# A hybrid encoder layer on one core: the first stage reordered by token tile and weight quarter, three latent units in full float32

## The chip, the core and the metric

The kernel runs on one core of one Trainium2 chip. The metric is the device time of one execution in microseconds (us), as the median of several runs; smaller is better. TensorE (PE in the profile, with its weight loads as PEld) multiplies, VectorE is DVE, ScalarE is ACT, GpSimd is POOL, and SyncE (SP) issues most of the loads. Each engine works through its own instructions in the order in which they are written, and waits at semaphores for the others.

## The reference, cut to what matters

One layer of a streaming encoder for 512 prompt tokens and 32 sample tokens, width 1024:

```python
xn = rms_norm(x, g_mix_norm)
z = xn @ w_in
c_q, c_kv, k_r, u, gate_a, gate_b = jnp.split(z, IN_SPLITS, axis=-1)   # 256, 128, 32, 1024, 1024, 1024
...
attn = chunk_causal_mla(q_nope, q_rope, k_nope, kr_all, v, q_pos, ...)
rec, h_last = rg_lru(u_c, h0, w_rg, b_rg, w_ig, b_ig, lru_lambda)
mixed = jax.nn.sigmoid(gate_a) * attn + jax.nn.sigmoid(gate_b) * rec
x = x + mixed @ w_out
up = rms_norm(x, g_ffn_norm) @ w_up
up_c, ffn_buf_new = causal_dwconv(up, ffn_buf, ffn_conv_w, ffn_conv_b)
gate, val = jnp.split(up_c, 2, axis=-1)
x = x + (jax.nn.silu(gate) * val) @ w_down
```

The first 416 columns of `w_in` give the latents (`c_q`, `c_kv`, `k_r`); only their product is touched here. `rg_lru` needs softplus(-lru_lambda), one small vector.

## The kernel before

Most products are made with three float32r matmuls in place of one float32 matmul: each operand is split into a high part (rounded to float32r) and a low part (the rest), and high x high, low x high and high x low are added up in PSUM. ACT makes the high parts and DVE the low ones by subtraction.

The first stage computes the latents of five token tiles: four of 128 prompt tokens and one that holds the 32 sample tokens. The product over the 1024 inputs runs in eight steps k of 128, and two steps share one load of weights, a weight quarter (128 x 832). A token tile times a weight quarter is called a unit here: twenty units, of 2 x 3 matmuls with 416 columns each. In `before.py` the stage goes so:

- SP (lines 386 to 412) issues the identity and the norm's gain, the five loads of `x` (512 KB for a prompt tile), weight quarters 0 and 1, thirteen loads of small vectors, and quarters 2 and 3, into `raw`. The weights of later items (512 KB) follow in `w_in_item`, each waiting for an earlier low split.
- PE transposes all of x tile by tile (`x_transpose`, line 1637), ACT and DVE each copy half of every tile to `xT` (`xT_left`, line 1142), and PE fills its wait with `keep_clock(7, 11)`, matmuls without use.
- ACT and DVE then split x times the gain, k by k over all tokens (`x_hi`, `x_lo`), and the weight quarters (`split_hi`, `split_lo`).
- PE multiplies quarter by quarter (line 1678), over all five tiles in each. After quarter 0 it transposes the small vectors (`vectors_transpose`), and after quarter 2 it spreads the inverse root mean squares over the partitions (line 1690).
- ACT's sums of squares of x (line 722) go to DVE, which makes the inverse roots (lines 1156 to 1157) and the diagonal tiles `dgx` (line 1159). The spread of them goes from PSUM to `rsT` (lines 1163 and 1164), and then `s_rs` is raised. After that comes the split of the first later item, and then the chain of 27 small instructions for softplus (lines 1171 to 1184).

The next stage on PE begins with

```python
pe.wait_ge(s_rs, 1)
pe.wait_ge(s_vec, 2)
for g, (kind, n) in enumerate(FIRST):
    ...
    product(xnh, xnl, g % 2, [(I_IN + g, I_IN + g, 0, KD)], None, early_keys(g), 5)
```

and `product` waits for the item's low split (`s_lo`). Everything later is released in turn from these products.

Of the kernel before, what the change touches and what calls it, by code (L numbers as in the profile page):

```python
# [15 lines left out]
F32 = mybir.dt.float32  # L16
# [4 lines left out]
P = 128  # L21

D = 1024
# [113 lines left out]
def layer(nc, i, c, o):  # L137
# [3 lines left out]
    with ctx:  # L141
# [33 lines left out]
        U = fixed("U", [P, KD, LEAD + TU])  # L175
        gates = fixed("gates", [P, 3, 2, T])
# [55 lines left out]
        lsq = at("lsq", [P, NTT, KVL + ROPE], zone + NTT * QL * 4)  # L232
        mxh = at("mxh", [P, KD, T], xs, F32R)
# [70 lines left out]

        def sem(name):
            return ctx.enter_context(nc.semaphore(name))
# [3 lines left out]
        s_xt = [sem(f"x{t}_in") for t in range(NTT)]  # L310
# [14 lines left out]
        s_xTd, s_xTa, s_xTv = sem("x_transposed"), sem("xT_left_half"), sem("xT_right_half")  # L325
# [59 lines left out]
        def _(sp):  # L385
            sp.dma_start(ident[:, :], c["ident"]).then_inc(s_ident, 16)
            sp.dma_start(vrows[V_GMIX:V_GMIX + 8, 0, :], i["g_mix_norm"].rearrange("a (m p) -> (a m) p", p=P)).then_inc(s_gain, 16)
            for t, (c0, p0, n) in enumerate(TOK):
                src = i["x_prompt"][0, c0:c0 + n, :] if t < NT else i["x_sample"][0]
                sp.dma_start(xnat[p0:, t, :], src).then_inc(s_xt[t], 16)  # L390
# [19 lines left out]

            latent_weights(2)
            latent_weights(3)
# [30 lines left out]

            for t in range(I_IN, I_IN + 11):
                w_in_item(t)
# [65 lines left out]
        def _(pool):  # L511
            step = Count(s_pool)

            pool.wait_ge(s_xt[NT], 16)
# [156 lines left out]
        def _(act):  # L671
# [5 lines left out]
            def split_hi(t, slot, loaded, n=KD * P):  # L677

                act.wait_ge(s_w[slot % 4], loaded)
                if not isinstance(t, int) or t >= 2:  # L680
                    act.wait_ge(s_used, t - 1)
                nc.scalar.activation(hi[:, slot % 2, 0:n], raw[:, slot % 4, 0:n], ACT.Copy).then_inc(s_hi, 1)  # L682
# [13 lines left out]
            def xT_left(t):  # L696
                c0, _, n = TOK[t]
                act.wait_ge(s_xTd, t + 1)
                nc.scalar.activation(xT[:, 0:4, c0:c0 + n], PS[:, 2 * (t % 2), :].rearrange("p (k n) -> p k n", k=4)[:, :, 0:n],
                                     ACT.Copy).then_inc(s_xTa, 1)  # L700

            def x_hi(dst, k, g0):

                nc.scalar.activation(dst[:, k, :], xT[:, k, :], ACT.Copy, scale=vec[:, g0 + k:g0 + k + 1]).then_inc(s_xh, 1)

            act.wait_ge(s_vecT, 1)
            nc.scalar.activation(vec[:, 0:8], PS[:, 6, 0:8], ACT.Copy).then_inc(s_vec, 1)
            for t in range(NTT):
                xT_left(t)
            act.wait_ge(s_vec, 1)  # L710
            act.wait_ge(s_xTa, NTT)
            act.wait_ge(s_xTv, NTT)
            for k in range(KD):
                x_hi(xnh, k, V_GMIX)
                if k in (0, 2):
                    split_hi(k // 2, k // 2, 16, 2 * LAT)

            act.wait_ge(s_cpre, 1)
            for t, (c0, p0, n) in enumerate(TOK):
# [3 lines left out]
                if t == 1:  # L723
                    split_hi(2, 2, 16, 2 * LAT)
# [4 lines left out]
            split_hi(3, 3, 16, 2 * LAT)  # L729
            split_hi(I_IN, I_IN, 32)  # L730
# [9 lines left out]
            split_hi(I_IN + 1, I_IN + 1, 32)  # L740
# [364 lines left out]
        def _(dve):  # L1105
# [34 lines left out]
            for t, (c0, _, n) in enumerate(TOK):  # L1140
                dve.wait_ge(s_xTd, t + 1)
                nc.vector.tensor_copy(xT[:, 4:8, c0:c0 + n], PS[:, 2 * (t % 2) + 1, :].rearrange("p (k n) -> p k n", k=4)[:, :, 0:n]).then_inc(s_xTv, 1)

            def x_lo(high, low, k, g0, count):

                dve.wait_ge(s_xh, count + k + 1)
                stt(low[:, k, :], xT[:, k, :], vec[:, g0 + k:g0 + k + 1], high[:, k, :].bitcast(F32), ALU.mult, ALU.subtract).then_inc(s_xl, 1)

            for k in range(KD):
                x_lo(xnh, xnl, k, V_GMIX, 0)  # L1150
                if k in (0, 2):
                    split_lo(k // 2, k // 2, 2 * LAT)
            split_lo(2, 2, 2 * LAT)
# [31 lines left out]


# [272 lines left out]
            split_item(I_IN + 1)  # L1459
# [81 lines left out]
            for m in range(KD):  # L1541
                x_m = xT[:, m, :]
                dve.wait_ge(s_used, I_OUT + m + 1)
                tt(halves(x_m), up_pair(m % 4), halves(x_m), ALU.add).then_inc(s_free, 1)
                dve.wait_ge(s_xh, KD + m + 1)
# [68 lines left out]
        def _(pe):  # L1614
# [22 lines left out]
            def x_transpose(t):  # L1637
                _, p0, n = TOK[t]
                pe.wait_ge(s_xt[t], 16)
                if t >= 2:  # L1640
                    pe.wait_ge(s_xTa, t - 1)
                    pe.wait_ge(s_xTv, t - 1)
                for k in range(KD):
                    last = nc.tensor.transpose(PS[:, 2 * (t % 2) + k // 4, (k % 4) * P:(k % 4) * P + n],  # L1644
                                               xnat[p0:, t, k * P:(k + 1) * P], ident[p0:, p0:])
                last.then_inc(s_xTd, 1)

            def vectors_transpose():

                pe.wait_ge(s_rows, 16 * 13)  # L1650
                pe.wait_ge(s_xTa, NT)
                pe.wait_ge(s_xTv, NT)
                for a, (c0, n) in enumerate(((0, V_N), (V_N, 2 * NU), (V_N + 2 * NU, 2 * NU), (V_N + 4 * NU, 2 * NU))):
                    last = nc.tensor.transpose(PS[:, 2, c0:c0 + n], vrows[0:n, a, :], ident[0:n, 0:n])
                last.then_inc(s_vecT, 1)

            pe.wait_ge(s_ident, 16)
            pe.wait_ge(s_gain, 16)
            nc.tensor.transpose(PS[:, 6, 0:8], vrows[0:8, 0, :], ident[0:8, 0:8]).then_inc(s_vecT, 1)
            for t in range(NTT):  # L1660
                x_transpose(t)
# [6 lines left out]
            keep_clock(7, 11)  # L1668

            for t4 in range(4):  # L1670
                pe.wait_ge(s_lo, t4 + 1)
                for kk, t in [(kk, t) for kk in range(2) for t in range(NTT)] if t4 < 3 else [(kk, t) for t in range(NTT) for kk in range(2)]:
                    k = 2 * t4 + kk
                    pe.wait_ge(s_xl, k + 1)
                    w0 = TOK[t][0] - TOK[t][1]
                    cols = slice(kk * LAT, (kk + 1) * LAT)
                    for w, x in ((hi, xnh), (hi, xnl), (lo, xnh)):
                        last = mm(PS[:, 3 + t, 0:LAT], x[:, k, w0:w0 + P], w[:, t4 % 2, cols],  # L1678
                                  start=(k == 0 and w is hi and x is xnh), stop=(k == KD - 1 and w is lo))
                    if t4 == 3 and t < NT and kk:  # L1680
                        last.then_inc(s_latp, 1)
                last.then_inc(s_used, 1)
                if t4 == 0:
                    vectors_transpose()
                if t4 == 2:

                    pe.wait_ge(s_rsn, 1)
                    for t, (c0, p0, n) in enumerate(TOK):
                        dst = PS[:, 0, c0:c0 + n] if t < NT else PS[:, 1, 0:n]
                        last = mm(dst, ones[:, :], dgx[:, t, p0:p0 + n], start=True, stop=True)  # L1690
                    last.then_inc(s_rsb, 1)
# [348 lines left out]
            for r in range(4):  # L2040
# [5 lines left out]
                product(x2h, x2l, r, [(I_UP + r, r, 0, KD)], (s_xl, KD) if r == 0 else None, x2_sums if r == 0 else None)  # L2046
# [109 lines left out]
```

## Time and profile before

| what | value |
|---|---|
| median of 3 runs | 859.44 us (859.42 to 859.92) |
| the profiled execution | 859.77 us |
| its span, first to last instruction | 857.5 us |
| PE busy | 841.3 us, 98% |
| DVE, ACT, POOL busy | 572.4, 365.2, 199.1 us |
| mean granted TensorE clock | 0.999 |

All times of rows are microseconds from the start of the span. The span leaves 2.3 us of the execution outside. A row of a group of instructions gives their busy time and the mean duration of one; a busy engine can start its next instruction before the record of the last has ended.

### The profile page before, as it was taken

How to read it: one execution, taken by the hardware profiler on the slowest of the kernel's cores; microseconds unless marked ns; L12 is line 12 of the kernel's file. 1: busy time of each engine (PE TensorE's matmuls, PEld its weight loads, DVE VectorE, ACT ScalarE, POOL GpSimd, SP SyncE). 2: the span in 40 equal slices, each digit the busy share in tenths (PEclk: the TensorE clock that was granted, in tenths of full speed). 3: DMA queues.
4: the chain of work that ended last, by engine and by line, in shares of the span. 5: the costliest groups of instructions: out<-in, count | busy, mean ns of one | idle time of the engine just before them, and what ended most of it. 6: DMA issues, size and time to landing. Idle time of an engine off the chain costs nothing.

```text
span 857.5 us, 16853 instructions
## 1 busy us (share of the span) xinstructions
PE 841.3 (98%) x6564; PEld 806.9 (94%) x6564; DVE 572.4 (67%) x1056; ACT 365.2 (43%) x608; POOL 199.1 (23%) x228
## 2 busy tenths in 40 slices
PE   7999999899999999999999999999999999999998
PEld 7999899789999899877999999999999999999998
DVE  5686678877676676887655888878888886222121
ACT  6635959755645556557245222222222221222121
POOL 4021123202111121121140444333442344010000
PEclk9999999999999999999999999999999999999999
DMA  8434211131120200100223233232323223233321
GB/s 256 112 91 109 78 51 39 40 81 38 33 58 18 53 26 28 50 2 26 75 75 99 74 99 92 79 98 73 98 79 92 86 79 93 83 106 103 105 57 40
DMA packets 114466, 63.73 MB, mean 74 GB/s; under 512 B 7660, under 2 KB 112878, under 8 KB 114412
## 3 DMA queue, kind: packets, MB, share of 16 engines
q1 hardware_dynamic: 112428, 59.25, 24.2%
q0 software_dynamic: 1936, 3.70, 1.7%
q8 instruction: 38, 0.62, 0.3%
q14 instruction: 16, 0.13, 0.0%
q10 hardware_dynamic: 48, 0.02, 0.0%
HBM read 59.85 MB, written 2.70 MB: 73 GB/s over the span
## 4 chain that ended last, share of the span: by engine, by line
PE 88%; ACT 6%; DVE 3%; issue 2%; DMA 0%; SPq 0%; ACTq 0%; DVEq 0%
PE PS L1632 49%; PE PS L1785 9%; PE PS L1868 6%; PE PS L1840 4%; PE PS L1802 4%; PE PS L1678 3%; PE PS L1744 2%; PE PS L1822 2%; PE PS L2075 2%; PE PS L1776 2%; PE PS L1740 1%; PE PS L1766 1%; PE PS L1707 1%; PE PS L1644 1%; PE PS L1847 1%
## 5 line engine op out<-in xcount | busy, mean ns | idle before, releaser
L682 ACT ACTIVATE w_hi<-w_raw 128x1024 fp32r<-128x1024 f32 (+2 forms) x102 | 105.4, 1034 | 301.4 <-PE PS L1632 288.8
L1115 DVE TENSOR_TENSOR w_lo<-w_raw,w_hi 128x1024 fp32r<-128x1024 f32 (+2 forms) x102 | 127.2, 1247 | 103.6 <-ACT w_hi L682 103.5
L1632 PE MATMUL PS<-x2h,w_hi 128*128 128x272 f32 x704 | 145.7, 288 | 0.0
L1632 PE MATMUL PS<-x2h,w_lo 128*128 128x272 f32 x704 | 145.7, 288 | 0.0
L1632 PE MATMUL PS<-x2l,w_hi 128*128 128x272 f32 x704 | 145.1, 288 | 0.0
L1632 PEld LDWEIGHTS PS<-x2h,w_hi 128*128 128x128 f32 x704 | 110.8, 188 | 0.1
L1632 PEld LDWEIGHTS PS<-x2l,w_hi 128*128 128x128 f32 x704 | 110.6, 189 | 0.0
L1632 PEld LDWEIGHTS PS<-x2h,w_lo 128*128 128x128 f32 x704 | 109.9, 189 | 0.0
L643 POOL TENSOR_TENSOR uct<-uct 128x512 f32<-128x512 f32 x22 | 28.4, 1292 | 165.0 <-DVE uct L1585 165.0
L1632 PE MATMUL PS<-hh,w_hi 128*128 128x272 f32 x308 | 64.2, 289 | 0.0
L1632 PE MATMUL PS<-hh,w_lo 128*128 128x272 f32 x308 | 63.8, 288 | 0.0
L1632 PE MATMUL PS<-hl,w_hi 128*128 128x272 f32 x308 | 63.5, 288 | 0.0
L1785 PE MATMUL PS<-xnh,w_hi 128*128 128x272 f32 x192 | 57.2, 298 | 0.2 <-DVE KT L1294 0.2
L1785 PE MATMUL PS<-xnh,w_lo 128*128 128x272 f32 x192 | 55.6, 290 | 0.0
L1785 PE MATMUL PS<-xnl,w_hi 128*128 128x272 f32 x192 | 55.2, 287 | 0.0
L901 ACT ACTIVATE PT<-PS 128x128 f32<-128x128 f32 (+4 forms) x72 | 31.3, 435 | 51.9 <-PE PS L1822 48.4
L574 POOL TENSOR_TENSOR rot<-Qn,rope 128x320 f32<-128x320 f32 x16 | 14.9, 949 | 160.5 <-DVE Qn L1284 160.5
L1802 PE MATMUL PS<-KT,QT 100*128 100x128 f32 (+3 forms) x128 | 46.9, 448 | 3.5 <-ACT Pn L887 2.2
L1632 PEld LDWEIGHTS PS<-hl,w_hi 128*128 128x128 f32 x308 | 48.4, 189 | 0.0
L1632 PEld LDWEIGHTS PS<-hh,w_hi 128*128 128x128 f32 x308 | 48.3, 188 | 0.1
L1632 PEld LDWEIGHTS PS<-hh,w_lo 128*128 128x128 f32 x308 | 48.1, 189 | 0.0
L1840 PE MATMUL PS<-PT,V 128*128 128x128 f32 x320 | 47.0, 278 | 0.0
(295 smaller groups left out, 1865.1 us busy)
## 6 DMA issues: line engine op xcount, KB each, us to landing
w_raw<-in_w_up_dram SPq DMA_DIRECT2D x44, 512.0 KB, 3.8
w_raw<-in_w_in_dram SPq DMA_DIRECT2D x24, 512.0 KB, 3.8
w_raw<-in_w_down_dram SPq DMA_DIRECT2D x16, 512.0 KB, 3.6
w_raw<-in_w_out_dram SPq DMA_DIRECT2D x8, 512.0 KB, 3.6
w_raw<-in_w_down_dram SPq DMA_DIRECT2D x8, 384.0 KB, 3.9
xnat<-in_x_prompt_dram SPq DMA_DIRECT2D x4, 512.0 KB, 5.0
w_raw<-in_w_in_dram SPq DMA_DIRECT2D x4, 416.0 KB, 6.5
wq<-in_w_q_b_dram SPq DMA_DIRECT2D x8, 192.0 KB, 2.5
```

Of the source, the lines that this page charges most:

```text
L643: nc.gpsimd.tensor_tensor(h_j[:, 0:SEQ], uct[:, j, 0:SEQ], h_j[:, 0:SEQ], ALU.mult)
L682: nc.scalar.activation(hi[:, slot % 2, 0:n], raw[:, slot % 4, 0:n], ACT.Copy).then_inc(s_hi, 1)
L901: nc.scalar.activation(PT[:, b, 0:w], PS[:, 6 + b, 0:w], ACT.Copy).then_inc(s_ptf, 1)
L1115: tt(lo[:, slot % 2, 0:n], raw[:, slot % 4, 0:n], hi[:, slot % 2, 0:n].bitcast(F32), ALU.subtract).then_inc(s_lo, 1)
L1632: last = mm(joined_half(2 * rank, j), w[:, slot % 2, cols], x[:, k0 + k, j * HT:(j + 1) * HT], start=(k0 + k == 0 and first), stop=(k0 + k ...
L1678: last = mm(PS[:, 3 + t, 0:LAT], x[:, k, w0:w0 + P], w[:, t4 % 2, cols], start=(k == 0 and w is hi and x is xnh), stop=(k == KD - 1 and w ...
L1744: last = mm(bank[:, a * 2 * QK:(a + 1) * 2 * QK], cqT[:, k, c0 - p0:c0 - p0 + P], wq[:, q % 2, k, :], start=(k == 0), stop=(k == NQ - 1))
L1776: last = mm(PS[:, bank, a * P:(a + 1) * P], latT[:, k0:k0 + P], wkv[:, q % 2, 1, :], start=True, stop=True)
L1785: last = mm(PS[:, j, 0:HT], w[:, item % 2, cols], x[:, k, j * HT:(j + 1) * HT], start=(k == 0 and first), stop=(k == KD - 1 and w is lo))
L1802: mm(bank[:, 0:w], QT[0:QK + NT, 2 * par + h, t * P:(t + 1) * P], KT[0:QK + NT, 2 * par + h, 0:w], start=True, stop=True).then_inc(s_s, 1)
L1840: last = mm(values_bank(h)[:, t * P:(t + 1) * P], V[:, par, a, h:h + 2, :].rearrange("p h n -> p (h n)"), PT[:, b, a * P:(a + 1) * P], sta ...
L1868: last = mm(PS[:, 2 * (r % 4) + j, 0:HT], w[:, cols], x[:, k, j * HT:(j + 1) * HT], start=(k == 0 and first), stop=(k == KD - 1 and w is w ...
```

## The change

The twenty units are ordered by tile and quarter, so that work starts on the first tile while the others load. x is first multiplied by the gain into `xg` (two tile slots) and split tile by tile, in seven parts: tiles 0 and 1 in halves, tiles 2, 3 and the sample tile whole. `xT` is filled by ACT alone (`x_kept`). The weight quarters have split tiles of their own (`lw_hi`, `lw_lo`). The three units (0,0), (1,0) and (0,1) (tile, quarter) multiply `xg` and `raw` in full float32, two matmuls each, and need no split. The two first later items are split ahead of the stage's end, and the copies to `rsT` come after softplus.

```diff
@@ SP
+            load_x(0, 0, D // 2)
             latent_weights(0)
+            load_x(0, D // 2, D)
+            load_x(1, 0, D // 2)
+            load_x(1, D // 2, D)
             latent_weights(1)
+            load_x(2)
+            latent_weights(2)
+            load_x(3)
+            load_x(4)
+            latent_weights(3)
...
+            sp.wait_ge(s_whole, 3)
             for t in range(I_IN, I_IN + 11):
                 w_in_item(t)
@@ ACT
+            def x_hi(part):
+                t, k0, k1 = XPARTS[part]
+                act.wait_ge(s_xg, part + 1)
+                nc.scalar.activation(x_tile(xnh, t, k0, k1), xg[:, t % 2, k0:k1, 0:TOK[t][2]], ACT.Copy).then_inc(s_xgh, 1)
+            def x_kept(t):
+                act.wait_ge(s_xTd, parts_of(t))
+                nc.scalar.activation(x_tile(xT, t, 0, KD), x_columns(t, 0, KD), ACT.Copy).then_inc(s_xTa, 1)
+            def latent_split_hi(q):
+                act.wait_ge(s_w[q], 16)
+                nc.scalar.activation(lw_hi[:, q, :], raw[:, q, 0:2 * LAT], ACT.Copy).then_inc(s_hi, 1)
...
+            x_hi(0)
+            latent_split_hi(0)
+            x_hi(1)
+            x_hi(2)
+            latent_split_hi(1)
+            x_hi(3)
+            x_kept(0)
+            x_kept(1)
+            x_hi(4)
+            latent_split_hi(2)
+            act.wait_ge(s_cpre, 1)
+            squares(0)
+            x_kept(2)
+            x_hi(5)
+            squares(1)
+            x_kept(3)
+            x_hi(6)
+            x_kept(4)
+            latent_split_hi(3)
+            for t in range(2, NTT):
+                squares(t)
+            split_hi(I_IN, I_IN, 32)
+            split_hi(I_IN + 1, I_IN + 1, 32)
@@ DVE
+            def x_scaled(part):
+                t, k0, k1 = XPARTS[part]
+                n = TOK[t][2]
+                dve.wait_ge(s_xTd, part + 1)
+                if t in (2, 3):
+                    dve.wait_ge(s_whole, 3)
+                gain = vec[:, V_GMIX + k0:V_GMIX + k1].unsqueeze(2).to_broadcast([P, k1 - k0, n])
+                tt(xg[:, t % 2, k0:k1, 0:n], x_columns(t, k0, k1), gain, ALU.mult).then_inc(s_xg, 1)
+            def x_lo(part):
+                t, k0, k1 = XPARTS[part]
+                dve.wait_ge(s_xgh, part + 1)
+                tt(x_tile(xnl, t, k0, k1), xg[:, t % 2, k0:k1, 0:TOK[t][2]], x_tile(xnh, t, k0, k1).bitcast(F32),
+                   ALU.subtract).then_inc(s_xgl, 1)
...
+            x_scaled(0)
+            x_lo(0)
+            x_scaled(1)
+            latent_split_lo(0)
+            x_scaled(2)
+            x_lo(2)
+            latent_split_lo(1)
+            x_scaled(3)
+            x_lo(1)
+            x_lo(3)
+            x_scaled(4)
+            x_lo(4)
+            latent_split_lo(2)
+            x_scaled(5)
+            x_lo(5)
+            x_scaled(6)
+            x_lo(6)
+            latent_split_lo(3)
...
-            split_lo(3, 3, 2 * LAT)
-            dve.wait_ge(s_rsb, 1)
-            nc.vector.tensor_copy(rsT[:, 0:SEQ], PS[:, 0, :])
-            nc.vector.tensor_copy(rsT[:, S0:], PS[:, 1, 0:DEC]).then_inc(s_rs, 1)
             split_lo(I_IN, I_IN)
+            split_lo(I_IN + 1, I_IN + 1)
 
             dve.wait_ge(s_spe, 1)
...
             ts(la_s[:, :], acc, -8.0, None, ALU.mult).then_inc(s_sp, 1)
 
+            dve.wait_ge(s_rsb, 1)
+            nc.vector.tensor_copy(rsT[:, 0:SEQ], PS[:, 0, :])
+            nc.vector.tensor_copy(rsT[:, S0:], PS[:, 1, 0:DEC]).then_inc(s_rs, 1)
@@ PE
+            def latent_product(t, q):
+                w0 = TOK[t][0] - TOK[t][1]
+                if t in (3, 4):
+                    pe.wait_ge(s_xg, parts_of(3))
+                    pe.wait_ge(s_xTa, 4)
+                for kk in range(2):
+                    k = 2 * q + kk
+                    pe.wait_ge(s_xgl, part_with(t, k) + 1)
+                    pe.wait_ge(s_hi, q + 1)
+                    cols = slice(kk * LAT, (kk + 1) * LAT)
+                    for w, x in ((lw_hi, xnh), (lw_hi, xnl), (lw_lo, xnh)):
+                        if w is lw_lo:
+                            pe.wait_ge(s_lo, q + 1)
+                        last = mm(PS[:, 3 + t, 0:LAT], x[:, k, w0:w0 + P], w[:, q, cols], ...)
...
+            def whole_latent_product(t, q):
+                pe.wait_ge(s_w[q], 16)
+                for kk in range(2):
+                    k = 2 * q + kk
+                    pe.wait_ge(s_xg, part_with(t, k) + 1)
+                    last = mm(PS[:, 3 + t, 0:LAT], xg[:, t, k, :], raw[:, q, kk * LAT:(kk + 1) * LAT], start=k == 0, stop=False)
+                last.then_inc(s_whole, 1)
...
+            keep_clock(5, 3)
+            x_transpose(0)
+            keep_clock(5, 2)
+            whole_latent_product(0, 0)
+            x_transpose(1)
+            keep_clock(5, 2)
+            x_transpose(2)
+            x_transpose(3)
+            whole_latent_product(1, 0)
+            whole_latent_product(0, 1)
+            latent_product(1, 1)
+            x_transpose(4)
+            latent_product(0, 2)
+            latent_product(1, 2)
+            for q in range(3):
+                latent_product(2, q)
+            x_transpose(5)
+            x_transpose(6)
+            for q in range(3):
+                latent_product(3, q)
+            vectors_transpose()
+            for t in range(4):
+                latent_product(t, 3)
+            latent_product(4, 0)
+            latent_product(4, 1)
+            x_rms_spread()
+            latent_product(4, 2)
+            latent_product(4, 3)
```

`x_transpose(part)` waits, from part 4 on, for the scaled parts and the kept copy (`s_xTa`) of the tile two before, because tiles 0, 2 and 4 share two PSUM banks and tiles 1 and 3 two others. Bank 6 of tile 3's columns is also the bank of its latents.

## Rows read from the trace of the kernel before

**Rows 1.** The page: busy time of the engines.
```profile
PE 841.3 (98%) x6564; PEld 806.9 (94%) x6564; DVE 572.4 (67%) x1056; ACT 365.2 (43%) x608; POOL 199.1 (23%) x228
```

**Rows 2.** The chain that ended last, 0 to 80 us: start, duration, what.
```profile
5.38 6.00 PE PS L1644 x32
...
15.12 5.91 PE PS L1678 x30
21.04 0.33 PE PS L1654 x4
21.37 11.33 PE PS L1678 x60
32.70 1.03 PE PS L1690 x10
...
39.49 6.01 PE PS L1632 x48
45.49 0.44 PE PS L1715 x4
...
74.56 1.85 PE PS L1707 x8
```

**Rows 3.** PE's timeline: start, duration, instructions.
```profile
2.90 0.24 PE L1659 MATMUL PS<-ident,vrows 8*128 8x8 f32 x1 [2.90 <-DMA vrows<-in_g_mix_norm_dram]
...
11.96 2.72 PE L1666 MATMUL PS<-ident 128*128 128x128 f32 x22
...
39.32 0.42 PE L1632 MATMUL PS<-xnh,w_hi 128*128 128x272 f32 x2
```

**Rows 4.** Stretches: length, busy (records) of PE, PEld, DVE, ACT, POOL, PEclk, DMA, GB/s.
```profile
5.00:10.00 5.00, 4.62 (x22) 4.62 (x23) 1.38 (x2) 1.19 (x2) 0.00 (x0) 1.00 1.04 361
...
10.00:11.00 1.00, 1.00 (x11) 1.00 (x10) 0.47 (x1) 0.47 (x1) 0.36 (x1) 1.00 1.02 379
```

**Rows 5.** Loads issued in two short stretches: KB, us from issue to landing.
```profile
xnat<-in_x_prompt_dram SPq DMA_DIRECT2D x1, 512.0 KB, 3.7
...
w_raw<-in_w_in_dram SPq DMA_DIRECT2D x1, 416.0 KB, 7.9
```

**Rows 6.** Groups by line and shape, 5 to 40 us: busy us, mean ns.
```profile
L1115 DVE TENSOR_TENSOR w_lo<-w_raw,w_hi 128x832 fp32r<-128x832 f32 x4 | 4.1, 1021 | 1.4 <-ACT w_hi L682 1.4
L682 ACT ACTIVATE w_hi<-w_raw 128x832 fp32r<-128x832 f32 x4 | 3.5, 887 | 0.7 <-PE PS L1678 0.7
...
L1142 DVE COPY xT<-PS 128x512 f32<-128x512 f32 x4 | 2.8, 692 | 8.3 <-PE PS L1644 8.3
...
L699 ACT ACTIVATE xT<-PS 128x512 f32<-128x512 f32 x4 | 2.4, 598 | 6.3 <-PE PS L1644 6.3
...
L1115 DVE TENSOR_TENSOR w_lo<-w_raw,w_hi 128x1024 fp32r<-128x1024 f32 x1 | 1.2, 1214 | 0.0
...
L682 ACT ACTIVATE w_hi<-w_raw 128x1024 fp32r<-128x1024 f32 x1 | 1.1, 1057 | 4.7 <-PE PS L1678 4.7
```

**Rows 7.** ACT's timeline, two sums of squares.
```profile
22.20 1.04 ACT L722 ACTIVATE junk<-xnat 128x1024 f32<-128x1024 f32 x1
...
23.36 1.06 ACT L722 ACTIVATE junk<-xnat 128x1024 f32<-128x1024 f32 x1
```

**Rows 8.** DVE's timeline from the squares to the first product's evacuation.
```profile
25.72 0.17 DVE L1156 TENSOR_SCALAR small<-small 128x5 f32<-128x5 f32 x1 [2.37 <-ACT junk L722]
...
27.93 1.07 DVE L1159 TENSOR_SCALAR dgx<-ident,small 128x128 f32<-128x128 f32 x5
...
35.61 0.19 DVE L1171 RECIPROCAL small<-la_s 128x8 f32<-128x8 f32 x1
...
40.94 0.17 DVE L1184 TENSOR_SCALAR la_s<-small 128x8 f32<-128x8 f32 x1
...
47.29 0.72 DVE L1453 TENSOR_TENSOR gates<-PS,rsT 128x544 f32<-128x544 f32 x1
```

**Rows 9.** PE's waits from 60 us on: us in total, times, longest.
```profile
PE PS L1802 <- ACT Pn L887: 2.2, 2, 1.2
```

More of the change, by code:

```diff
@@ L175, in layer @@
         U = fixed("U", [P, KD, LEAD + TU])
+        gates_at = place
         gates = fixed("gates", [P, 3, 2, T])
@@ L303, in score_bank, with parts_of, part_with, x_columns @@
             return PS[:, 2 + 2 * ((p + n) % 2), :]
+        XPARTS = [(0, 0, 4), (0, 4, 8), (1, 0, 4), (1, 4, 8)] + [(t, 0, 8) for t in range(2, NTT)]
+        def parts_of(t):
+            return sum(part[0] <= t for part in XPARTS)
+        def part_with(t, k):
+            return [k0 <= k < k1 and tile == t for tile, k0, k1 in XPARTS].index(True)
+        def x_columns(t, k0, k1):
+            bank = 6 if t in (1, 3) else 0
+            return PS[:, bank:bank + 2, :].rearrange("p a (k n) -> p (a k) n", k=4)[:, k0:k1, 0:TOK[t][2]]
+        def x_tile(x, t, k0, k1):
+            c0, _, n = TOK[t]
+            return x[:, k0:k1, c0:c0 + n]
         def sem(name):
@@ L309, in layer @@
         s_gain = sem("mix_gain_in")
-        s_xt = [sem(f"x{t}_in") for t in range(NTT)]
+        s_xt = [sem(f"x{t}_{k0}_in") for t, k0, _ in XPARTS]
         s_w = [sem(f"w{s}_in") for s in range(4)]
@@ L693, in rsqrt_guess, with squares @@
                 nc.scalar.activation(dst, dst, ACT.Exp, scale=-0.5).then_inc(sem_, 1)
[L696 to L719, printed above, removed]
+            def x_hi(part):
[8 more added lines that the diff above has]
+                nc.scalar.activation(lw_hi[:, q, :], raw[:, q, 0:2 * LAT], ACT.Copy).then_inc(s_hi, 1)
+            def squares(t):
+                _, p0, _ = TOK[t]
                 if t:
@@ L1138, in _, with latent_split_lo @@
             nc.vector.memset(small[0:LASTP, 2, NT:NTT], 1.0).then_inc(s_cpre, 1)
[L1140 to L1153, printed above, removed]
+            def x_scaled(part):
[11 more added lines that the diff above has]
+                   ALU.subtract).then_inc(s_xgl, 1)
+            def latent_split_lo(q):
+                dve.wait_ge(s_hi, q + 1)
+                tt(lw_lo[:, q, :], raw[:, q, 0:2 * LAT], lw_hi[:, q, :].bitcast(F32), ALU.subtract).then_inc(s_lo, 1)
+            dve.wait_ge(s_vec, 1)
+            x_scaled(0)
[16 more added lines that the diff above has]
+            latent_split_lo(3)
             dve.wait_ge(s_ss, NTT)
@@ L1458, in _ @@
             link(nc.vector.tensor_reduce(small[:, 0, 2 * NTT:3 * NTT], lsq[:, :, KVL:], X, ALU.add))
-            split_item(I_IN + 1)
             latent_norms()
@@ L1634, in product, with x_transpose, keep_clock @@
                     last.then_inc(s_used, 1)
-            def x_transpose(t):
+            def x_transpose(part):
+                t, k0, k1 = XPARTS[part]
                 _, p0, n = TOK[t]
-                pe.wait_ge(s_xt[t], 16)
+                pe.wait_ge(s_xt[part], 16)
                 if t >= 2:
+                    pe.wait_ge(s_xg, parts_of(t - 2))
                     pe.wait_ge(s_xTa, t - 1)
[L1642 to L1645, printed above, removed]
+                for k in range(k0, k1):
+                    last = nc.tensor.transpose(x_columns(t, k, k + 1)[:, 0], xnat[p0:, t, k * P:(k + 1) * P], ident[p0:, p0:])
                 last.then_inc(s_xTd, 1)
+            def keep_clock(bank, count):
+                for _ in range(count):
+                    mm(PS[:, bank, 0:P], ident[:, :], ident[:, :], start=True, stop=True)
             def vectors_transpose():
                 pe.wait_ge(s_rows, 16 * 13)
-                pe.wait_ge(s_xTa, NT)
-                pe.wait_ge(s_xTv, NT)
+                pe.wait_ge(s_vec, 1)
                 for a, (c0, n) in enumerate(((0, V_N), (V_N, 2 * NU), (V_N + 2 * NU, 2 * NU), (V_N + 4 * NU, 2 * NU))):
@@ new lines, in whole_latent_product, with x_rms_spread @@
+            def whole_latent_product(t, q):
[5 more added lines that the diff above has]
+                last.then_inc(s_whole, 1)
+            def x_rms_spread():
+                pe.wait_ge(s_rsn, 1)
+                for t, (c0, p0, n) in enumerate(TOK):
+                    dst = PS[:, 0, c0:c0 + n] if t < NT else PS[:, 1, 0:n]
+                    last = mm(dst, ones[:, :], dgx[:, t, p0:p0 + n], start=True, stop=True)
+                last.then_inc(s_rsb, 1)
@@ L1657, in _ @@
             pe.wait_ge(s_ident, 16)
             pe.wait_ge(s_gain, 16)
-            nc.tensor.transpose(PS[:, 6, 0:8], vrows[0:8, 0, :], ident[0:8, 0:8]).then_inc(s_vecT, 1)
-            for t in range(NTT):
-                x_transpose(t)
-            def keep_clock(bank, count):
-                for _ in range(count):
-                    mm(PS[:, bank, 0:P], ident[:, :], ident[:, :], start=True, stop=True)
[L1668 to L1691, printed above, removed]
```

40 lines of the change are left out of this document (25 added, 15 removed).

## The prediction

> **What bounds the kernel now.** First the page's busy times: PE is busy 98% of the span [rows 1], so a change of this stage is worth what it does to the moment at which PE starts the next one. Then the chain that ended last, over the first 80 us. The reader is to see that it hardly leaves PE: transposes of x from 5.38, the latent products from 15.12, the small vectors and the spread of the inverse roots between them, and the products of the later items behind that [rows 2]. PE's timeline shows the two places where PE isn't at useful work: up to 5.38 it waits for x, and from 11.96 it runs 22 records of filler until the first splits are there [rows 3]. The first product of the next stage starts at 39.32 [rows 3]. That is the number to forecast for the changed kernel. The later waits on PE are short, the longest 1.2 us [rows 9], and all are for ACT and DVE work that is itself released by PE's products, so a shift of this start goes to the end nearly whole.
>
> From 15.12 to 39.32 PE has no gap. 120 matmuls take 22.8 us, 0.19 each (11.33 us for 60), so a unit of six takes 1.13 us; the vectors take 0.33 and the spread 1.03 [rows 2]. What the change can save is only the filler and the low clock ahead of 15.12. What it can lose is every place where in-order queues now make PE wait for a split.
>
> **Prices.** A transpose of 128 columns takes 0.11 us (0.44 for 4) [rows 2], but 22 took 4.62 us between 5 and 10 us, 0.21 each, and from 10 to 11 us there were 11 [rows 4]. The granted clock reads 1.00 in both stretches, yet equal work ran at half pace: the first is TensorE's lower level, 1.2 GHz, the second 2.4 GHz. Between the start at 5.38 and the change of pace lie about 4.7 us of unbroken work. A filler matmul is 2.72/11 = 0.25 us [rows 3], 0.5 at the low level.
>
> A float32 matmul of 416 columns isn't in the trace. Four float32 products of about 272 columns take 1.85 us, 0.46 each [rows 2]; by columns that gives 0.70. The two bounds are 3 x 0.19 = 0.57 (no dearer than the split) and 0.25 x 416/128 = 0.81 (by the filler). I take 0.70: a whole unit is 1.4 us against 1.13, so the three cost PE 0.8 us more, and 17 split units stay, 19.2 us.
>
> On DVE 512 elements from PSUM take 0.69 and 1024 elements 1.21 [rows 6]. The gain multiply reads PSUM and a repeated gain, which the trace lacks: 0.69 and 1.2, with 0.6 and 1.35 as ends. On ACT 512 elements take 0.60 and 1024 take 1.0 to 1.06; a latent quarter takes 0.89 on ACT and 1.02 on DVE [rows 6]. A sum of squares comes every 1.16 us [rows 7].
>
> The first 512 KB of x landed 3.7 us after issue [rows 5]. It is now 256 KB: the last 256 KB took 0.6 us or so at the measured 361 GB/s [rows 4], so it lands 0 to 0.7 us earlier than 5.3. I take 4.7. Quarter 0 is issued next; the bound is what quarter 1 took before, behind 2.5 MB, 7.9 us [rows 5], and the likely value some 1.2 us behind x, about 6.0. No other load is late: even with the longest delay each lands 1 us or more before its use below, except the second half of tile 1, due near 10.
>
> **The stage worked out.** All starts are in us from the span's start.
>
> - To 8.5. Filler after the gain's transpose at 2.9 [rows 3] to 4.6. Half tile 0 is transposed 4.7 to 5.6 at 0.21 each, its record ends at 5.75, the gain multiply ends at 6.5. Two fillers end at 6.5. Unit (0,0) in float32 starts there. If the clock rises 4.7 us after work began at 3.1, at 7.8, 1.3 us at half pace do 0.65 of the 1.4, and it ends at 8.55. Were the rise as late as 10.1, everything behind comes 1.2 later; at 6.6, 0.5 earlier.
> - To 14.2. Second half of tile 0, filler and tile 1 end at 10.4. Unit (1,0) needs DVE's third gain multiply, and DVE has before it the second (9.1 to 9.75) and quarter 0's low split (to 10.7): 11.4. PE waits 1.0. Units (1,0) and (0,1) end at 14.2.
> - Unit (1,1) needs three `x_lo`, the third in DVE's order is `x_lo(1)`. ACT: `x_hi(2)` to 12.0, quarter 1 to 12.9. DVE: quarter 1's low part to 13.9, the fourth gain multiply to 14.5, `x_lo(1)` to 15.15. PE waits 0.95 and multiplies to 16.3.
> - Tile 2's transposes, 16.3 to 17.2. The next unit, (0,2), needs quarter 2 split, and ACT makes that split only behind `x_hi(4)`, which needs the gain multiply of the very tile just transposed: DVE to 18.5, `x_hi(4)` to 19.6, quarter 2's high part to 20.4. DVE's low part stands behind `x_lo(4)`: 20.8, 21.8. PE waits 3.2, does two matmuls, and waits 1.0 for the third.
> - The rest of (0,2) (0.75) and four units (4.5) end at 27.1, tile 3's transposes at 27.95, the sample tile's at 28.45. Unit (3,0) writes bank 6, where tile 3's columns stand until `x_kept(3)`. ACT gets there after: gain multiply on DVE to 29.3, `x_hi(5)` to 30.35, `squares(1)` to 31.5, `x_kept(3)` to 32.5. PE waits 4.05.
> - PE then has 11 units (12.4), the vectors (0.33) and the spread (1.03): 46.3.
> - ACT goes on after 32.5 with the sample tile (0.6), quarter 3 (0.85) and three sums of squares (3.5): 37.4. DVE's chain from the sums to `dgx` is 25.72 to 29.0, 3.3 us [rows 8]: 40.7. Then come two splits of 1024 (2.3): 43.0. Softplus took from 35.61 to 41.1, 5.5 us [rows 8], and now lies ahead of the copies to `rsT`: 48.5. The copies (0.8) end at 49.2. PE, done at 46.3, waits 2.9 for `s_rs`.
>
> So the first product starts at 49.2 where it was 39.3: +9.9 us. PE's waits after 10.4 sum to 13.1 us (1.0, 0.95, 3.2, 1.0, 4.05, 2.9). The profiled execution took 859.77 us, 0.33 above the median of 859.44. 859.77 + 9.9 = 869.7 on the first scale, **869.3 us** on the second.
>
> Costed at nothing: SP's wait for the whole units ends at 14.2, and the item behind it is needed for ACT's split at 37.4, 23 us later; the queue behind it is paced by low splits as before. The item in raw slot 3 waits for quarter 3's low split, about 35, and is multiplied after three later products of 6.01 us each [rows 2]. The small vectors, issued behind all x and quarters, are needed at 36. GpSimd's constants wait for the sample tile, some 2 us later than before, and are used after 50. Were any of these covers gone, PE would wait at the place named by what the load is late.
>
> **The rivals.**
>
> *The clock falls in the gaps.* Row first: before the change PE has no wait over 1.2 us after its start [rows 9], and equal work took twice the time only at the start [rows 4], so the trace can't show whether waits of 3.2 + 1.0, 4.05 and 2.9 us cost the clock. If they do, a low stretch as long as the first, 4.7 us, does 2.35 us less work. In the first gap that delays tile 3's transposes and all behind them, 871.7; in the second it is hidden under DVE's chain (46.3 + 2.4 < 49.2); in the last it falls on the first product. One decides: 871.7; two: 874. For it speaks that idle is most of 17.2 to 21.8; against it that each gap is barely as long as the first ramp. The Trainium skill's page "TensorE: Matmul & The Clock Gate", section "HAM oscillation — how this bites in real kernels", says that an engine left waiting between groups of matmuls is throttled again and starts the next group cold. By it the sum would be 871.7 rather than 869.3; no row of the kernel before shows such a fall.
>
> *Later slack gives some back.* DVE evacuates the first product at 47.29, 1.8 us after it ended at 45.50 [rows 2, 8], because splits, softplus and norms were queued up. Now softplus and both splits are behind it when the product starts. If that lead of 1.8 us reaches waits such as the 2.2 us for ACT [rows 9], the time is 867.5. Against: those waits come 60 us later behind many products.
>
> *PE doesn't wait (the other side).* If the splits keep ahead of PE from 15.15 on, 17 units (19.2), the transposes left (2.2), vectors and spread (1.4) end at 38.0, 1.3 us before 39.3: 858.1. It decides if quarter 2 is split both ways by 17.2, 4.6 us before my 21.8, and tile 3 kept by 28.4. For it: the loads are there. Against: ACT's and DVE's queues are in order, and the transposes on which `x_hi(4)` rests end only at 17.2.
>
> *No net change.* The gain is eaten exactly by a part of the waits; that needs them to sum to about 1.3 instead of 13.1.
>
> **How the numbers follow.** Forecast as worked out, 0.64; clock falls, 0.20; slack gives back, 0.10; no waits, 0.04; no net change, 0.02. The likeliest case has its own range by the clock's rise (-0.5, +1.2) and the multiply's ends (some 0.8 either way on the four on the path with their followers): 868.0 to 871.0. With the clock case at one fall and the slack case the range is 867.0 to 872.5. Within 0.2% (1.7 us) is about what a measurement here can tell from no change. Faster 0.04, same 0.02, slower 0.94.
>
> **What would show it.** Float32 matmuls of 416 columns at 0.70 us the pair of records; PE waiting for quarter 2's high part at about 17 and for its low part at 21; a wait for `xT` near 28.5 to 32.5, with a sum of squares inside; `rsT` copied after softplus near 49 and the first product right after; transposes at 0.11 after each gap (0.21 would be the clock's fall). A first product near 38 would say that the queues run ahead of PE, and the step to doubt would be the one at 17.2.

## The result, and the profile after

The changed kernel takes 872.14 us (median of 4 runs, 871.35 to 873.33), the kernel before 859.68 beside it. The ratio is 1.0145, with a 95% interval of 1.0133 to 1.0158: 12.5 us slower. The forecast was 869.3, in a range of 867.0 to 872.5; the measured median lies in it, near the upper end, and two of the four runs (872.53 and 873.33) lie above it. The profiled execution took 871.76 us.

The page of the changed kernel, the busy times to hold against [rows 1], and the granted clock in 40 slices:

```profile
span 869.4 us, 16867 instructions
PE 846.6 (97%) x6550; PEld 808.2 (93%) x6550; DVE 576.3 (66%) x1057; ACT 365.1 (42%) x607; POOL 198.5 (23%) x228
...
PEclk9799999999999999999999999999999999999999
```

PE is busy for 5.3 us more and the span is 11.9 us longer. PEclk shows a 7 in the second slice, where it was 9 throughout before.

PE's timeline of the changed kernel: the last record of the latents and the first product of the next stage, which stood at 39.32 in [rows 3].

```profile
50.91 0.35 PE L1755 MATMUL PS<-lw_lo,xnh 128*128 128x416 f32 x1
51.10 0.45 PE L1711 MATMUL PS<-xnh,w_hi 128*128 128x272 f32 x2
```

The stage ends 11.8 us later. Behind it nothing changed: from the first product to the end of the span it is 857.5 - 39.32 = 818.2 us before and 869.4 - 51.10 = 818.3 us now. So the whole loss lies in this stage.

What PE waited for in the first 60 us of the changed kernel (total, times, longest):

```profile
PE PS L1755 <- ACT xT L742: 3.8, 1, 3.8
...
PE PS L1755 <- ACT lw_hi L747: 3.3, 1, 3.3
...
PE PS L1768 <- DVE xg L1201: 1.4, 2, 1.1
...
PE PS L1755 <- DVE xnl L1207: 0.6, 1, 0.6
...
PE PS L1755 <- DVE lw_lo L1213: 0.3, 1, 0.3
```

And the chain that ended last, which now leaves PE again and again, where [rows 2] hardly leave it:

```profile
13.42 0.60 DVE xg L1201
14.02 0.61 DVE xnl L1207
...
14.68 1.41 PE PS L1755 x6
16.09 0.89 PE PS L1725 x8
...
17.00 1.24 DVE xg L1201
...
18.25 1.06 ACT xnh L737
...
20.48 1.03 DVE lw_lo L1213
...
21.56 7.77 PE PS L1755 x28
29.33 0.89 PE PS L1725 x8
...
30.24 1.23 DVE xg L1201
...
31.50 1.06 ACT xnh L737
32.55 1.04 ACT junk L754 x2
33.59 0.92 ACT xT L742
```

The reader is to see the two detours. Behind tile 2's transposes (16.09) come the gain multiply, `x_hi(4)` and the low part of quarter 2, until PE can go on at 21.56. Behind tile 3's (29.33) come the gain multiply, `x_hi(5)`, a sum of squares that PE has no use for there, and `x_kept(3)`.

The stretches of 2 us around both (columns as in [rows 4]) show what followed each detour:

```profile
17.00:19.00 2.00, 0.00 (x0) 0.00 (x0) 1.22 (x1) 0.75 (x1) 2.00 (x5) 1.00 1.41 325
19.00:21.00 2.00, 0.76 (x2) 0.50 (x2) 1.66 (x2) 2.00 (x4) 2.00 (x4) 0.65 0.74 74
21.00:23.00 2.00, 1.72 (x5) 1.39 (x5) 0.50 (x1) 1.04 (x3) 2.00 (x5) 0.50 0.76 206
...
25.00:27.00 2.00, 2.00 (x9) 1.93 (x8) 0.00 (x0) 0.00 (x0) 0.66 (x2) 0.64 0.99 292
...
35.00:37.00 2.00, 2.00 (x7) 1.91 (x7) 1.29 (x2) 1.97 (x5) 0.00 (x0) 0.50 0.00 0
```

The granted clock fell to half, 1.2 GHz, in both gaps. By these rows, as (1 - clock) x 2 us / 0.5 for each, the first low stretch is 1.4 us of 19 to 21, all of 21 to 25 and 1.4 us of 25 to 27: 6.8 us. The matmuls of 416 columns in it start every 0.35 us, not every 0.19.

DVE's timeline of the changed kernel, with the rows that answer to [rows 8]:

```profile
39.29 0.17 DVE L1236 TENSOR_SCALAR small<-small 128x5 f32<-128x5 f32 x1 [2.37 <-ACT junk L754]
...
42.49 2.35 DVE L1168 TENSOR_TENSOR w_lo<-w_raw,w_hi 128x1024 fp32r<-128x1024 f32 x2
44.76 0.19 DVE L1248 RECIPROCAL small<-la_s 128x8 f32<-128x8 f32 x1
...
50.80 0.18 DVE L1265 COPY rsT<-PS 128x32 f32<-128x32 f32 x1
```

The copies to `rsT` end at 51.0, and PE is through its last unit at 51.1. Two chains end at the same moment here, so the record of waits shows none for `rsT`, though taking time from PE alone would gain next to nothing.

### The profile page after: what moved, and what is told of

Read it like the earlier page. It is cut to its first block, busy times and chain, and to the rows that moved or that the text cites. A ratio compares the mean times of both kernels' runs of the same rounds, so it can differ in the third digit from the quotient of the medians.

```text
span 869.4 us, 16867 instructions
## 1 busy us (share of the span) xinstructions
PE 846.6 (97%) x6550; PEld 808.2 (93%) x6550; DVE 576.3 (66%) x1057; ACT 365.1 (42%) x607; POOL 198.5 (23%) x228
## 4 chain that ended last, share of the span: by engine, by line
PE 87%; ACT 7%; DVE 4%; issue 2%; DMA 0%; SPq 0%; ACTq 0%; DVEq 0%
PE PS L1711 49%; PE PS L1903 8%; PE PS L1986 6%; PE PS L1958 4%; PE PS L1920 4%; PE PS L1755 3%; PE PS L1862 2%; PE PS L1940 2%; PE PS L2193 2%; PE PS L1894 2%; PE PS L1858 1%; PE PS L1884 1%; PE PS L1825 1%; DVE xg L1201 1%; PE PS L1965 1%
## 5 line engine op out<-in xcount | busy, mean ns | idle before, releaser
L719 ACT ACTIVATE w_hi<-w_raw 128x1024 fp32r<-128x1024 f32 (+1 forms) x98 | 101.8, 1040 | 298.9 <-PE PS L1711 291.5
L1168 DVE TENSOR_TENSOR w_lo<-w_raw,w_hi 128x1024 fp32r<-128x1024 f32 (+1 forms) x98 | 124.1, 1267 | 102.8 <-ACT w_hi L719 102.8
```

Source lines behind the costliest of these rows:

```text
L1168: tt(lo[:, slot % 2, 0:n], raw[:, slot % 4, 0:n], hi[:, slot % 2, 0:n].bitcast(F32), ALU.subtract).then_inc(s_lo, 1)
```

## The experiments

Each ran beside the kernel before, 4 to 11 times. Times are medians; the difference is to the kernel before on the same chip.

| label | us | kernel before | difference, ratio (95%) | first product |
|---|---|---|---|---|
| the change | 872.14 | 859.68 | +12.5, 1.0145 (1.0133 to 1.0158) | 51.10 |
| fill_both | 869.45 | 860.11 | +9.3, 1.0109 (1.0094 to 1.0125) | 48.94 |
| fill_first | 870.05 | 860.11 | +9.9, 1.0116 (1.0100 to 1.0131) | 49.26 |
| fill_second | 871.52 | 860.11 | +11.4, 1.0132 (1.0116 to 1.0147) | 51.45 |
| quarter2_early | 867.78 | 860.11 | +7.7, 1.0091 (1.0077 to 1.0104) | 46.33 |
| fill_both_rs_early | 867.21 | 859.78 | +7.4, 1.0082 (1.0069 to 1.0096) | 47.69 |
| tile3_early | 869.92 | 859.78 | +10.1, 1.0118 (1.0103 to 1.0134) | 47.17 |
| reordered | 859.44 | 859.78 | -0.3, 0.9996 (0.9987 to 1.0005) | 39.06 |
| reordered_split | 858.17 | 859.78 | -1.6, 0.9981 (0.9972 to 0.9990) | 37.68 |
| after_split | 870.60 | 859.80 | +10.8, 1.0120 (1.0105 to 1.0134) | 50.57 |
| tile3_sample_early | 865.27 | 859.80 | +5.5, 1.0061 (1.0045 to 1.0077) | 42.73 |

The last column is PE's first product of the next stage in the profiled execution, which can lie up to 2.3 us from the median run. From there to the end of the span it is 818.0 to 818.4 us in all of them but tile3_early (819.7).

**What the low clock costs.** Three kernels put filler into PE's two long waits and change nothing else.

```diff
             x_transpose(4)
+            keep_clock(5, 12)    # fill_both, fill_first
...
             x_transpose(6)
+            keep_clock(2, 14)    # fill_both, fill_second
```

> The changed kernel with 12 filler matmuls (0.25 us each, 3.0 us) in PE's wait behind tile 2's transposes and 14 (3.5 us) in the wait behind the sample tile's transposes; orders, splits and loads unchanged. Theory: the granted clock of 0.50 after both waits goes, the first wait's fall cost some 2 us on the path, the second was hidden behind the DVE chain that ends with the copies to rsT. The first product starts near 49.0 instead of 51.1, the clock row stays at 1.00, time 870.0 (-2.1). Rival (the low clock lies off the path, only the waits for the splits count): first product at 51.1, 872.1.

> Only the 12 fillers in the first wait. Theory: the fall after the second wait remains but is hidden: PE ends its latents at about 49.0, the copies to rsT end then too, first product near 49.1, time 870.1, as fill_both. Rival (each fall costs its 2.4 us): the second fall counts as well and the time is 2.4 us above fill_both.

> Only the 14 fillers in the second wait. Theory: PE's latent products end 2.4 us earlier, near 48.7, and then PE waits for the copies to rsT, whose chain is unchanged: first product at 51.0, time 872.0, no gain. Rival (each fall costs its 2.4 us): first product at 48.7, time 869.7.

fill_both is 2.7 us faster than the change, its clock row reads 1.00, and the first product comes at 48.94. fill_first has nearly all of it, 870.05, with the second fall still there. fill_second is at 871.52, 0.6 us under the change (1.1 by the differences to before, and inside the spread of the change's runs). PE's first product names what held it, first in fill_both, then in fill_second:

```profile
48.94 0.52 PE L1711 MATMUL PS<-xnh,w_hi 128*128 128x272 f32 x2 [2.28 <-DVE rsT L1265]
```
```profile
51.45 0.52 PE L1711 MATMUL PS<-xnh,w_hi 128*128 128x272 f32 x2 [2.30 <-DVE rsT L1265]
```

So the fall in the first wait costs 2.1 us of the 12.5 by the medians (2.5 by the differences to before), and the second is hidden behind the DVE chain: the time PE got back became a wait for `rsT`. The size of the second is read in fill_both, where the work from unit (3,0) to the end of the latents takes 14.2 us (32.50 to 46.66) against 16.5 in the change (34.60 to 51.10): 2.3 us. The 2.30 us of fill_second are not that price alone, for its first units came 1.2 us later and its low stretch after the first wait was 3.4 us long and not 6.8. The rival by which each fall costs its price is out, and so is the one by which neither counts.

**The order of quarter 2.**

```diff
 ACT             x_kept(0)
+            latent_split_hi(2)
             x_kept(1)
             x_hi(4)
-            latent_split_hi(2)
...
 DVE             x_lo(3)
+            latent_split_lo(2)
             x_scaled(4)
             x_lo(4)
-            latent_split_lo(2)
```

> ACT's high part of weight quarter 2 moved ahead of x_kept(1) and x_hi(4), DVE's low part ahead of x_scaled(4); nothing else. Theory (the queue order is the cause): the wait of 3.3 us for quarter 2 becomes one of about 0.4, another of about 1.3 us appears ahead of tile 2's units, the first clock fall goes with the wait, tile 3's transposes come near 24.3 instead of 29.2, and the first product near 46.4: 867.4 (-4.7). Rival (PE is bound there by loads or by the sum of ACT's and DVE's work, so that the wait only moves): within 1 us of 872.1.

867.78 us, 4.4 us under the change (by medians; 4.8 by the differences to before), and the first product at 46.33 where 46.4 was expected. PE's waits between 5 and 60 us in it:

```profile
PE PS L1755 <- ACT xT L742: 3.8, 1, 3.8
PE PS L1755 <- DVE xnl L1207: 1.9, 2, 1.3
...
PE PS L1755 <- DVE lw_lo L1213: 0.2, 1, 0.2
```

The wait of 3.3 us for `lw_hi` is gone and 1.3 us in front of tile 2's units is new, as worked out. The loads and the sum of work were not the bound; one pair of lines in two queues was. The 4.4 us hold the first clock fall as well: the granted clock is 1.00 from 17 to 27 us in this kernel.

**The place of the copies to rsT.** In fill_both, their three lines were put back between the two splits and softplus.

```diff
             split_lo(I_IN + 1, I_IN + 1)
+            dve.wait_ge(s_rsb, 1)
+            nc.vector.tensor_copy(rsT[:, 0:SEQ], PS[:, 0, :])
+            nc.vector.tensor_copy(rsT[:, S0:], PS[:, 1, 0:DEC]).then_inc(s_rs, 1)
```

> fill_both (fillers in both waits), and the copies to rsT put back ahead of softplus. Theory: with the clock held, PE's latents end at 46.7 and the wait of 2.3 us for rsT is the place of softplus in DVE's order: first product at 46.7, time 2.3 us under fill_both, 9.3 us under the change's 12.5 above before, so +7.1 us against before. Rival (what holds rsT is the chain of squares, inverse roots and splits, not softplus): within 0.5 us of fill_both.

867.21 against 869.45: 2.2 us for a reordering on DVE alone, where PE's wait for `rsT` had been 2.3. The wait is in none of PE's rows any more. (The profiled execution, 868.07, was the slowest of the five; its second float32 unit began 1.3 us later than the change's, at 12.35 and not 11.06, because the first ran longer at the low clock.)

**Tile 3's transposes.** Two kernels move transposes up.

```diff
             x_transpose(4)
+            x_transpose(5)          # both
             latent_product(0, 2)
             latent_product(1, 2)
+            x_transpose(6)          # tile3_sample_early
...
-            x_transpose(5)          # both
-            x_transpose(6)          # tile3_sample_early
```

> The changed kernel with tile 3's transposes right behind tile 2's, instead of behind tile 2's units; everything else in its order. Theory: the second wait (3.8 us) and its clock fall go, ACT's tail (tile 3, quarter 3, squares) starts some 7 us earlier, and so does softplus; the first wait for quarter 2 stays at about 2.5 to 3.3 us. First product near 43.7, +4.4 us against before. Rival (ACT and DVE have no room and tile 3's split delays quarter 2 and tile 2): first product above 48, more than +8.5 us.

The expectation was wrong. The second wait did go, but the time is 869.92, +10.1 against 4.4 expected. The rival's time fits (above +8.5), but its first product (above 48, measured 47.17) and its mechanism don't: quarter 2 came no later than in the change (its first matmul at 20.17, there 20.24). ACT's timeline of tile3_early shows what was late next, and PE's shows where it ended:

```profile
30.52 0.42 ACT L737 ACTIVATE xnh<-xg 128x256 fp32r<-128x256 f32 x1 [4.91 <-DVE xg L1201]
30.84 0.37 ACT L742 ACTIVATE xT<-PS 128x256 f32<-128x256 f32 x1
31.10 0.89 ACT L747 ACTIVATE lw_hi<-w_raw 128x832 fp32r<-128x832 f32 x1
31.89 1.05 ACT L754 ACTIVATE junk<-xnat 128x1024 f32<-128x1024 f32 x1
```
```profile
29.34 0.68 PE L1725 MATMUL PS<-ident,xnat 32*128 32x32 f32 x8
...
47.17 0.82 PE L1711 MATMUL PS<-xnh,w_hi 128*128 128x272 f32 x2 [3.04 <-DVE rsT L1265]
```

The sample tile's transposes still stood behind tile 2's units, and ACT's whole tail (quarter 3, the last sums of squares, and so DVE's chain to `rsT`) stood behind `x_hi(6)`: ACT sat idle 4.91 us for a tile of 32 tokens. PE then waited 3.04 us for `rsT`, the clock fell in that wait, and the first product ran at half pace, which is the 819.7 in place of 818.2.

> tile3_early with the sample tile's transposes moved up too, behind unit (1,2). Theory (in tile3_early ACT's tail was held by x_hi(6), whose transposes stood behind tile 2's units): the sample tile's transposes at about 25.5 instead of 29.3, the last sum of squares ends near 31.3, the copies to rsT near 43.0, and PE ends its units at 43.9 without a wait: first product at 43.9, +4.6 us against before. Rival (the tail is bound by ACT's and DVE's own work): within 1 us of tile3_early, +9 to +10.

With the sample tile moved up too, the time is 865.27, +5.5 (862.74 to 867.09), and PE waits neither for `xT` nor for `rsT`: the chain runs on PE alone from 21.6 to 85.9. The profile has the first product at 42.73 where 43.9 was expected, and the median is 0.9 us above the expectation. Its six runs fall apart by mean clock: two at 0.994 took 866.35 and 867.09, four at 0.998 or 0.999 took 862.74 to 865.49. A step of 0.004 is about 3.5 us of lost work, so the low stretches were longer in the two slower runs; the wait of 2.41 us for quarter 2, which this kernel keeps, is the one that brings the low clock in the profiled run. The 2.7 us between the four others the mean clock doesn't show.

**The whole order, and the float32 units.** `reordered` keeps the float32 units and all loads, and reorders the three queues from tile 2's transposes on.

```diff
 ACT  x_kept(0), latent_split_hi(2), x_kept(1), latent_split_hi(3), x_hi(4), x_kept(2), squares(0),
      x_hi(5), x_kept(3), x_hi(6), x_kept(4), squares(1) to squares(4)
 DVE  latent_split_lo(2), x_scaled(4), latent_split_lo(3), x_lo(4), x_scaled(5), x_lo(5), x_scaled(6), x_lo(6),
      and the copies to rsT ahead of softplus
 PE   x_transpose(4), (0,2), x_transpose(5), (1,2), (0,3), (1,3), x_transpose(6), (2,0..3), (3,0..3),
      vectors_transpose(), (4,0), (4,1), x_rms_spread(), (4,2), (4,3)
```

> The changed kernel, the three float32 units kept, its queues reordered: quarters 2 and 3 split ahead of tile 2's and tile 3's parts, tile 3 transposed between (0,2) and (1,2), units (0,3) and (1,3) before tile 2's, rsT copied ahead of softplus. Theory (the stage by tile and quarter isn't slow by itself, the order of its in-order queues is): PE has no wait over 0.6 us after 14.7, first product at 38.0, 1.3 us earlier than before the change: time -1.3 us against before. Rival (the form itself costs: three float32 units and 23 us of ACT and DVE work ahead of the stage's end): first product later than 39.3, time above before.

859.44 against 859.78: 12.7 us of the change's loss is gone by order alone, with the same float32 units, splits and loads. PE's waits from 5 to 60 us are what the theory left:

```profile
PE PS L1767 <- DVE xg L1200: 1.1, 1, 1.1
PE PS L1754 <- DVE xnl L1206: 0.6, 1, 0.6
PE PS L1754 <- DVE lw_lo L1212: 0.2, 1, 0.2
```

But of the 1.3 us of gain expected over before, 0.3 came, and the interval (0.9987 to 1.0005) holds no change. In its profile the first float32 unit ran at the low clock for most of its time, 2.26 us of records where the change's took 1.64 (from its start to the next instruction 2.09 and 1.47):

```profile
6.55 2.26 PE L1767 MATMUL PS<-w_raw,xg 128*128 128x416 f32 x4
...
39.06 0.41 PE L1710 MATMUL PS<-xnh,w_hi 128*128 128x272 f32 x2
```

That is 0.6 us of the 1.1 by which the first product (39.06) came later than expected (38.0). The other 0.5 lies between unit (1,1) at 15.27 and the first product: 23.8 us where 23.3 were reckoned.

`reordered_split` and `after_split` replace the three float32 units by split ones, in the new order and in the change's.

```diff
-            whole_latent_product(0, 0)
             x_transpose(1)
             keep_clock(5, 2)
             x_transpose(2)
             x_transpose(3)
-            whole_latent_product(1, 0)
-            whole_latent_product(0, 1)
+            split_unit(0, 0)      # latent_product(0, 0).then_inc(s_whole, 1)
+            split_unit(1, 0)
+            split_unit(0, 1)
```

Two more fillers stand where unit (0,0) was, and DVE splits quarter 0 ahead of `x_scaled(1)`. One more thing differs, which the expectations don't name. DVE makes `x_lo(2)` ahead of `x_lo(1)`, and the change's `latent_product` counts parts, so that unit (1,1), which reads only `x_lo(2)`, waits for the third `x_lo` as well: 0.58 us. The two kernels without float32 wait for the right count (`XL_COUNT`), and DVE's gain multiply of tiles 2 and 3 waits for the four `x_lo` before it.

> As reordered, but the three float32 units are made of split matmuls as the other seventeen, multiplied behind tile 1's transposes; DVE splits quarter 0 ahead of the second gain multiply. Theory (the float32 units cost PE 0.28 us each more and free nothing that the path waits for, since the splits are made all the same): unit (1,1) ends 0.5 to 1.2 us earlier and the first product comes 0.5 to 1.2 us before that of reordered. Rival (the float32 units are what lets PE start before the splits): 0.5 to 1.5 us later than reordered.

> The changed kernel with its three float32 units made of split matmuls, multiplied behind tile 1's transposes, quarter 0 split on DVE ahead of the second gain multiply; the rest of every queue as in the change. Theory (the float32 units are a small part of the loss, some 1.2 us, as between reordered and reordered_split): everything from tile 2's transposes on comes 1.2 us earlier, first product near 49.9, +11.3 us against before. Rival (float32 is the cause of the loss): below +6 us. Second rival (without float32 units PE starts late and loses): above +12.5 us.

Without float32 the reordered kernel is 1.3 us faster, 858.17, and 1.6 us faster than before the change (0.9981, 0.9972 to 0.9990): the one version that beats both kernels, by 0.19%. In the change's own order the same edit gives 870.60, 1.5 us less (1.7 by the differences). PE starts its first unit later and still ends (1,1) earlier: tile 2's transposes begin at 15.06 in reordered_split, after 16.52 in reordered and 15.92 in the change. Both rivals of after_split are out: float32 is neither the cause of the loss nor what saves a late start. But the 1.3 to 1.7 us are the price of the float32 form with its waits, not of its multiplications alone: those are 3 x 0.28 = 0.84, and no run has float32 units with the right count.

The form without float32 is also the steadier one. Ten of the eleven runs of reordered_split lie between 857.97 and 858.30, while those of reordered spread from 858.84 to 860.11. The profiles point at unit (0,0), which stands where the clock first rises. PE runs the same instructions up to it in all nine kernels with float32 units, yet from its start to the next instruction it took 1.47 us in the change, 2.53 in fill_second and 2.77 in fill_both_rs_early:

```profile
6.58 1.64 PE L1768 MATMUL PS<-w_raw,xg 128*128 128x416 f32 x4 [0.29 <-DVE xg L1201]
```
```profile
6.57 2.93 PE L1768 MATMUL PS<-w_raw,xg 128*128 128x416 f32 x4
```

All that follows is later by as much, 1.3 us at most. So a profiled first product of the table holds up to 1.3 us that say nothing of the order of the queues.

## Why the prediction was right, point by point

- *The start of the next stage sets the time.* Right: all but one of the kernels have 818.0 to 818.4 us behind it. The rival of later slack is out, for DVE's lead gave nothing back: 818.3 us behind the start, 818.2 before the change.
- *Up to 14.2.* Right within 0.5 us. Half tile 0 was transposed from 4.51 (4.7 predicted). The wait for the third gain multiply was 1.09 (1.0 predicted), that for `x_lo(1)` 0.58 (0.95). A float32 matmul of 416 columns took 0.71 us (four in 3.03, less the end of the last record), 0.70 predicted. The clock's first rise was forecast at 7.8; fillers at 5.4 ran at half pace and the float32 unit at 6.58 at full, so it came near 6.4. It is no fixed moment: in other runs of the same instructions it came as late as 9.2 (worked out from the 2.77 us of fill_both_rs_early), between the two ends that the prediction gave (6.6 and 10.1).
- *Quarter 2.* The wait of 3.2 us was 3.28, for the instruction named. The wait for the low part was 0.28, not 1.0, in part because the two matmuls before it ran at half the clock: at full clock, in fill_both, it was 0.70.
- *Tile 3 and bank 6.* 4.05 us predicted, 3.79 measured, with the sum of squares inside it.
- *The tail.* From the last square to the end of `rsT` 11.8 us were predicted (37.4 to 49.2) and 11.7 measured (39.29 to 50.98). (By its own terms the sum ends at 49.3, and 256 KB at 361 GB/s are 0.7 us, not 0.6; neither matters.)
- *The clock holds in the gaps.* This step failed. It had the likeliest case's 0.64 behind it; the case in which the clock falls had 0.20, and its 871.7 for one fall on the path is what came (872.14). The forecast number was off by 2.8 us, mostly for this reason, and the range held it only because it had been stretched for that case: the likeliest case by itself ended at 871.0. The granted clock fell to 0.50 in both gaps. The fall in the first, on the path, cost 2.1 to 2.5 us. The second was hidden as forecast ("46.3 + 2.4 < 49.2"), though only just: the two chains ended 0.1 us apart. The price of 2.35 us came out by some luck, for it stood on a low stretch of 4.7 us, and the stretch was 6.8 us long, of which PE spent a part waiting. And fill_both, in which the clock is held, gives back the likeliest case: first product 48.94 (49.2 predicted), +9.3 us (+9.9 predicted). The rule of the Trainium skill's page "TensorE: Matmul & The Clock Gate", section "HAM oscillation — how this bites in real kernels", was the better guide here than the lack of rows, and this case's trace agrees with it: 0.50 after waits of 3.28 and 3.79 us. The kernel before had no wait after its start long enough to show a fall.
- *PE doesn't wait, 858.1.* Out for the change. It is what the same parts can do in another order: reordered came to 859.44 with float32 units, reordered_split to 858.17.

By the experiments the order of the queues is the whole 12.5 us, for reordered takes them all back with its float32 units in place. Of them quarter 2's place is 4.8 us, in which the first clock fall has 2 to 2.5; most of the rest is the tail of tile 3, sample tile, squares and softplus. These parts overlap, and no run measures the whole tail by itself. The float32 units with their waits cost 1.3 to 1.7 us beside that, in reordered too.

What stays open: the change's four runs spread over 2.0 us at one mean clock (0.992). The moment of the first rise can make 1.3 us of that, and the granted clock would not show it, but only one of the four has a trace. The runs of tile3_sample_early spread over 4.4 us, in part with the mean clock. Why a rise comes later or a fall lasts longer in one run than in another no run here shows.

## What to carry to other kernels

When a stage is cut into tiles so that it can start early, write down for every unit of the bound engine which split it needs and what stands ahead of that split in its in-order queue; one weight split behind one tile's split cost 4.8 us here. A piece that is tiny on one engine (32 sample tokens) can hold the whole tail of another, so move it with the big ones, and look again for what is late next before pricing the gain. Every wait of 2.41 us or more on TensorE after its start brought the low clock here, so price a new wait of that size with a fall, 2.1 to 2.5 us in this case where it lay on the path.

## What the runs showed of the hardware

- A wait of 2.41 us on PE, from 17.76 to 20.17, was enough for the clock to fall (tile3_early: the granted clock is 0.72 from 19 to 21 us and 0.50 from 21 to 25, and the first matmul after the wait runs at half pace), while waits of 2.28 and 2.30 us (fill_both, fill_second) were followed by a clock of 1.00. PE's row in tile3_early:

```profile
20.17 0.69 PE L1755 MATMUL PS<-lw_hi,xnh 128*128 128x416 f32 x1 [2.41 <-ACT lw_hi L747]
```

- The low stretches weren't equally long: 6.8 us in the change, 3.4 us in fill_second after the same wait. The ten of all traces are 6.8 us in six cases (both of the change and of after_split, that of fill_first, the first of tile3_early) and 3.4 in four. The rows of fill_second give its stretch, as (1 - clock) x 2 us / 0.5 summed. They also show that the fall can come after the wait: it ended at 21.42, and the clock fell near 22.5.

```profile
21.00:23.00 2.00, 0.87 (x3) 0.56 (x4) 1.68 (x2) 2.00 (x4) 2.00 (x4) 0.87 0.65 196
23.00:25.00 2.00, 2.00 (x7) 1.90 (x8) 0.00 (x0) 0.23 (x1) 2.00 (x5) 0.50 0.81 220
25.00:27.00 2.00, 2.00 (x10) 1.96 (x9) 0.00 (x0) 0.00 (x0) 0.87 (x2) 0.78 1.12 333
```

- The granted clock reads 1.00 ahead of the first rise even where equal work runs at half pace, so that the first low stretch has to be read from the pace of equal instructions (in the kernel before, 22 transposes of 128 columns took 4.62 us between 5 and 10 us, and 11 of them 1.00 us from 10 to 11, at 1.00 both times).
